# Products of high and low parts, ordered by kind within each group of twelve

## What is computed

```python
def first_block(x, ...):                      # layer 1
    h = rms_norm(x, norm_mix_g)
    proj = h @ w_in                           # 1024 -> 8280 columns
    ...
    merged = sigmoid(gate_a) * o_gdn + sigmoid(gate_b) * o_att
    x = x + merged @ w_out                    # gated delta rule and sparse attention before it
    h2 = rms_norm(x, norm_mlp_g)
    x = x + square(relu(h2 @ w_mlp_up)) @ w_mlp_down
# layer 2: x = x + (retention and forgetting attention) @ w_out,
#          x = x + cross attention to a memory (w_xq, w_xkv, w_xo),
#          x = x + (gated MLP with w_gate, w_up, w_down)
```

## Time and profile before

| what | value |
|---|---|
| median of three runs | 920.71 us (919.72 to 921.14) |
| the profiled execution's own time | 920.04 us |
| its span, first to last instruction | 918.2 us |
| time around the span | 1.8 us |
| TensorE matmuls busy | 899.7 us, 98% of the span |
| TensorE weight loads busy (beside matmuls) | 766.8 us, 84% |
| DVE, ACT, POOL busy | 586.3, 447.9, 113.5 us |
| the 16 DMA engines' mean busy share | about 50% (q1 48.0%) |
| granted TensorE clock, mean over the span | 1.000 |

### The profile page before, as it was taken

The page is one execution under the profiler, slowest core; times in us unless marked ns, Lnnn a source line. Parts: engine busy times, 40 slices in busy tenths (PEclk is TensorE's granted clock), DMA queues, the critical chain, the costliest instruction groups (busy, mean ns, idle before and its releaser), DMA issues.

```text
span 918.2 us, 12609 instructions
## 1 busy us (share of the span) xinstructions
PE 899.7 (98%) x5039; PEld 766.8 (84%) x5039; DVE 586.3 (64%) x834; ACT 447.9 (49%) x632; POOL 113.5 (12%) x83
## 2 busy tenths in 40 slices
PE   8999999999999999999999999999999999999998
PEld 6887787888978999988878889888877888888886
DVE  5378978996686566644356747877765565554542
ACT  6265446854545555533344336545553454444431
POOL 0331225756110000000000002100100000000200
PEclk9999999999999999999999999999999999999999
DMA  8774542344235555555567535524440565554562
GB/s 279 200 249 138 183 138 81 130 123 115 91 102 175 172 181 180 187 190 188 183 202 272 190 94 185 183 93 138 173 148 18 168 195 188 188 183 143 188 220 69
DMA packets 83554, 149.74 MB, mean 163 GB/s; under 512 B 8480, under 2 KB 16208, under 8 KB 83376
## 3 DMA queue, kind: packets, MB, share of 16 engines
q1 hardware_dynamic: 80352, 144.55, 48.0%
q10 hardware_dynamic: 2528, 3.63, 1.1%
q0 software_dynamic: 624, 0.87, 0.8%
HBM read 147.59 MB, written 1.44 MB: 162 GB/s over the span
## 4 chain that ended last, share of the span: by engine, by line
PE 83%; DVE 10%; ACT 3%; DMA 2%; issue 1%; POOL 0%; DVEq 0%; SPq 0%; ACTq 0%
PE gemm L504 21%; PE gemm L506 20%; PE gemm L505 20%; DMA raw<-in_w_in_dram 2%; PE mixbank L642 2%; DVE mix L1893 2%; PE mixbank L617 2%; PE gemm L946 2%; PE mixbank L946 2%; PE gemm L948 2%; PE mixbank L947 2%; PE mixbank L948 2%; PE gemm L947 2%; DVE w_lo L1664 2%; PE mixbank L520 1%
## 5 line engine op out<-in xcount | busy, mean ns | idle before, releaser
L1664 DVE TENSOR_TENSOR w_lo<-raw,w_hi 128x2048 fp32r<-128x2048 f32 (+3 forms) x131 | 284.7, 2183 | 190.6 <-ACT w_hi L1152 190.5
L1152 ACT ACTIVATE w_hi<-raw 128x2048 fp32r<-128x2048 f32 (+3 forms) x140 | 255.2, 1832 | 177.3 <-DMA raw<-in_w_in_dram 51.7
L504 PE MATMUL gemm<-w_hi,s_hi 128*128 128x512 f32 (+3 forms) x784 | 302.5, 386 | 6.4 <-DVE s_lo L1701 2.8
L506 PE MATMUL gemm<-w_hi,s_lo 128*128 128x512 f32 (+3 forms) x784 | 296.0, 378 | 0.0
L505 PE MATMUL gemm<-w_lo,s_hi 128*128 128x512 f32 (+3 forms) x784 | 295.7, 377 | 0.0
L504 PEld LDWEIGHTS gemm<-w_hi,s_hi 128*128 128x128 f32 x784 | 147.5, 188 | 35.9 <-issue 6.8
L506 PEld LDWEIGHTS gemm<-w_hi,s_lo 128*128 128x128 f32 x784 | 147.3, 188 | 27.4
L505 PEld LDWEIGHTS gemm<-w_lo,s_hi 128*128 128x128 f32 x784 | 147.5, 188 | 26.0 <-issue 0.5
L2398 POOL TENSOR_TENSOR sm<-sm 128x2 f32<-128x2 f32 (+4 forms) x13 | 22.7, 1749 | 498.0 <-DVE sm L1708 315.1
L2392 POOL TENSOR_TENSOR w_lo<-raw,w_hi 128x2048 fp32r<-128x2048 f32 x9 | 41.3, 4604 | 158.7 <-ACT w_hi L1152 158.7
L504 PE MATMUL gemm<-w_hi,hT_hi 128*128 128x512 f32 x128 | 50.6, 396 | 0.0
(11 more groups left out here) (333 smaller groups left out, 1190.7 us busy)
## 6 DMA issues: line engine op xcount, KB each, us to landing
raw<-in_w_in_dram SPq DMA_DIRECT2D x40, 1024.0 KB, 5.0
raw<-in_w_mlp_up_dram SPq DMA_DIRECT2D x16, 1024.0 KB, 5.3
raw<-in_w_mlp_down_dram SPq DMA_DIRECT2D x16, 1024.0 KB, 5.1
raw<-in_w_gate_dram SPq DMA_DIRECT2D x10, 1024.0 KB, 5.1
raw<-in_w_up_dram SPq DMA_DIRECT2D x10, 1024.0 KB, 5.0
raw<-in_w_down_dram SPq DMA_DIRECT2D x10, 1024.0 KB, 5.0
raw<-in_w_out_dram SPq DMA_DIRECT2D x8, 1024.0 KB, 5.0
raw<-in_w_xkv_dram SPq DMA_DIRECT2D x8, 1024.0 KB, 5.2
```

Source lines behind the costliest of these rows:

```text
L504: nc.tensor.matmul(o, hi, wh, start=kt == 0, stop=False)
L506: last = nc.tensor.matmul(o, lo, wh, start=False, stop=kt == blk["kt"] - 1)
L1152: nc.scalar.activation(w_hi[:, n % SLOTS, 0:kn, 0:width], raw[:, n % SLOTS, 0:kn, 0:width], ACT.Copy)\
L1664: V.tensor_tensor(w_lo[:, s, 0:kn, 0:width], raw[:, s, 0:kn, 0:width], w_hi[:, s, 0:kn, 0:width].bitcast(F32), ALU.subtract)\
```

## The change

Only TensorE's stream is changed; every matmul of before is still there, with the same operands, and the loads and the streams of ACT, DVE, POOL and SP are the same.

- In `mm`, with activations just turned (`turned`): the pair waits for `w_hi` (`split_hi` or `first_hi`) and for `turn_hi`, makes its four x_hi w_hi; then waits for `w_lo` and makes its four x_hi w_lo; then waits for `turn_lo` and makes its four x_lo w_hi.
- In `mm` otherwise: at a chunk's first pair it waits for `split_hi`, makes four x_hi w_hi and four x_lo w_hi, then waits for `w_lo` and makes four x_hi w_lo. The hidden activations' low parts are waited for at the start, as before.
- The last pair of the blocks in `EARLY` keeps the order of before.
- In the first `up`, the first chunk is done in two groups of 24 (each pair of k tiles with four column tiles), with the kinds in order and with waits for `turn_hi` and `turn_lo`; it still waits for `w_lo` at its start.

```diff
--- before.py
+++ after.py
@@ -484,28 +484,63 @@
                     c = 2 * pair // CK
                     n = blk["chunk0"] + c
                     kn, width = chunk_shape(b, c)
-                    if b == 0:
-                        pe.wait_ge(sem("split_lo" if pair % 2 else "first_lo"), c + 1)
-                    elif 2 * pair == CK * c:
-
-                        pe.wait_ge(sem("split_lo_pool" if pool_chunk(b, c) else "split_lo"), at(low_parts(b, c), 4, i))
-                    if turned is not None:
-
-                        pe.wait_ge(sem("turn_lo"), turned - KT // 2 + pair + 1)
-                    if hidden is not None:
-
-                        pe.wait_ge(sem(hidden), pair + 1)
                     early = b in EARLY and 2 * pair == blk["kt"] - 2
                     tiles = [(kt, t) for kt in (2 * pair, 2 * pair + 1) for t in range(NT)]
-                    for kt, t in sorted(tiles, key=lambda tile: tile[1]) if early else tiles:
-                        o = G[b % 2][t][:, 0:width]
-                        hi, lo = (s[:, kt, P * t:P * t + P] for s in stat)
-                        wh, wl = (s[:, n % SLOTS, kt - CK * c, 0:width] for s in (w_hi, w_lo))
-                        nc.tensor.matmul(o, hi, wh, start=kt == 0, stop=False)
-                        nc.tensor.matmul(o, hi, wl, start=False, stop=False)
-                        last = nc.tensor.matmul(o, lo, wh, start=False, stop=kt == blk["kt"] - 1)
-                        if early and t == 0 and kt == blk["kt"] - 1:
-                            last.then_inc(sem("first_tile"), 1)
+
+                    def product(kt, t, low_x=False, low_w=False):
+
+                        lhs = stat[low_x][:, kt, P * t:P * t + P]
+                        rhs = (w_lo if low_w else w_hi)[:, n % SLOTS, kt - CK * c, 0:width]
+                        return nc.tensor.matmul(G[b % 2][t][:, 0:width], lhs, rhs, start=kt == 0 and not (low_x or low_w),
+                                                stop=kt == blk["kt"] - 1 and (low_x if ends_low_x else low_w))
+
+                    def low_weights():
+
+                        if b == 0:
+                            pe.wait_ge(sem("split_lo" if pair % 2 else "first_lo"), c + 1)
+                        elif 2 * pair == CK * c:
+                            pe.wait_ge(sem("split_lo_pool" if pool_chunk(b, c) else "split_lo"), at(low_parts(b, c), 4, i))
+
+                    ends_low_x = True
+                    if turned is not None:
+                        if b == 0:
+                            pe.wait_ge(sem("split_hi" if pair % 2 else "first_hi"), c + 1)
+                        elif 2 * pair == CK * c:
+                            pe.wait_ge(sem("split_hi"), n + 1)
+                        pe.wait_ge(sem("turn_hi"), turned - KT // 2 + pair + 1)
+                        for kt, t in tiles:
+                            product(kt, t)
+                        low_weights()
+                        for kt, t in tiles:
+                            product(kt, t, low_w=True)
+                        pe.wait_ge(sem("turn_lo"), turned - KT // 2 + pair + 1)
+                        for kt, t in tiles:
+                            last = product(kt, t, low_x=True)
+                    elif early:
+                        low_weights()
+                        if hidden is not None:
+
+                            pe.wait_ge(sem(hidden), pair + 1)
+                        for kt, t in sorted(tiles, key=lambda tile: tile[1]):
+                            product(kt, t)
+                            product(kt, t, low_w=True)
+                            last = product(kt, t, low_x=True)
+                            if t == 0 and kt == blk["kt"] - 1:
+                                last.then_inc(sem("first_tile"), 1)
+                    else:
+                        ends_low_x = False
+                        if 2 * pair == CK * c:
+                            pe.wait_ge(sem("split_hi"), at(n + 1, 4, i))
+                        if hidden is not None:
+
+                            pe.wait_ge(sem(hidden), pair + 1)
+                        for kt, t in tiles:
+                            product(kt, t)
+                        for kt, t in tiles:
+                            product(kt, t, low_x=True)
+                        low_weights()
+                        for kt, t in tiles:
+                            last = product(kt, t, low_w=True)
                     if kt == CK * c + kn - 1:
                         last.then_inc(sem("mm_done"), 1)
 
@@ -939,20 +974,34 @@
                     pe.wait_ge(sem("ev0"), at(B_UP + b - 1, 2, i))
                     pe.wait_ge(sem("ev1"), at(B_UP + b - 1, 2, i))
 
+                def tile_product(kt, f, low_x=False, low_w=False):
+                    n = blocks[B_UP + b]["chunk0"] + kt // CK
+                    w = (w_lo if low_w else w_hi)[:, n % SLOTS, kt % CK, P * f:P * f + P]
+                    return nc.tensor.matmul(UP_BANKS[b % 2][f][:, 0:SEQ], w, (s_lo if low_x else s_hi)[:, kt, :],
+                                            start=kt == 0 and not (low_x or low_w), stop=kt == KT - 1 and low_x)
+
                 def tile_products(kt, f):
-                    n = blocks[B_UP + b]["chunk0"] + kt // CK
-                    o = UP_BANKS[b % 2][f][:, 0:SEQ]
-                    wh, wl = (w[:, n % SLOTS, kt % CK, P * f:P * f + P] for w in (w_hi, w_lo))
-                    nc.tensor.matmul(o, wh, s_hi[:, kt, :], start=kt == 0, stop=False)
-                    nc.tensor.matmul(o, wl, s_hi[:, kt, :], start=False, stop=False)
-                    return nc.tensor.matmul(o, wh, s_lo[:, kt, :], start=False, stop=kt == KT - 1)
+                    tile_product(kt, f)
+                    tile_product(kt, f, low_w=True)
+                    return tile_product(kt, f, low_x=True)
 
                 pe.wait_ge(sem("split_lo"), at(low_parts(B_UP + b, 0), 4, i))
-                for kt in range(CK):
-                    if first and kt % 2 == 0:
-                        pe.wait_ge(sem("turn_lo"), 12 - KT // 2 + kt // 2 + 1)
-                    for f in range(4):
-                        last = tile_products(kt, f)
+                if first:
+
+                    for pair in range(CK // 2):
+                        tiles = [(kt, f) for kt in (2 * pair, 2 * pair + 1) for f in range(4)]
+                        pe.wait_ge(sem("turn_hi"), 12 - KT // 2 + pair + 1)
+                        for kt, f in tiles:
+                            tile_product(kt, f)
+                        for kt, f in tiles:
+                            tile_product(kt, f, low_w=True)
+                        pe.wait_ge(sem("turn_lo"), 12 - KT // 2 + pair + 1)
+                        for kt, f in tiles:
+                            last = tile_product(kt, f, low_x=True)
+                else:
+                    for kt in range(CK):
+                        for f in range(4):
+                            last = tile_products(kt, f)
                 last.then_inc(sem("mm_done"), 1)
                 pe.wait_ge(sem("split_lo"), at(low_parts(B_UP + b, 1), 4, i))
                 if first:
```

## The result

The changed kernel takes **912.93 us** (median of 912.50, 912.81, 913.05 and 914.11); before, four runs on the same chip gave a median of 920.92. The ratio is 0.9921, with a 95% interval of 0.9909 to 0.9933: 7.3 us faster, between 6.2 and 8.4. (The two medians alone differ by 8.0, inside that interval.) The forecast was 913.6 us with a range of 911.0 to 917.0. The profiled execution took 913.05 us with a span of 911.3 (forecast 912.9 and 911.1), against 918.2 before.

A forecast was written before the change was run, and what follows sets the result against it. TensorE, with matmuls busy 98% of the span, bounds the kernel. Stalls won, 5.04 + 2.26 - 0.2 = 7.1 us, take the profiled 920.04 to 912.9; the runs' median lies 0.67 higher, so 913.6 us, range 911.0 to 917.0.

The forecast's parts named there:

- What one stall costs: On TensorE, a stall costs its idle time plus 0.16 us of row overlap, used behind transposes too.
- low activations: At seven TensorE waits for `s_lo`, stalls go whole except at 275.27, where 0.82 is won; 5.04 us in sum.
- Low weights: At two TensorE waits for `w_lo`, 1.11 us is won at 47.76 and 1.15 at 110.58; 2.26 in sum.
- What lies behind: Loads and later work move forward with TensorE; only about 0.2 us is lost in the first attention groups.
- Edits that cost nothing: In TensorE's stream, 161 more waits, alternating banks and neighbours without a shared stationary x_hi cost 0.
- The sum: Over the whole kernel, 5.04 + 2.26 - 0.2 = 7.1 us is won.
- Rival 1: Gains before the attention groups (120 to 262 us) are swallowed: 2.9 us lost, 4.2 left, 916.5 us; chance 0.12.
- Rival 2: Each added wait at a group's fifth and ninth matmul costs; at 0.07 us each, 924.9 us; chance 0.04.
- Rival 3: Matmul distance depends on order: 930.1 us if slower (chance 0.04), 908.4 if faster in MLP down projections (0.03).
- Rival 4: Only one kind of stall is won; without low weights, 915.7 us; chance 0.07, shared with no difference for unseen reasons.

The follow-up runs named there:

- Experiment 1: Kernel before with the new order and waits only for just turned activations (first up block included); 915.25 us, ratio 0.9945.
- Experiment 2: Kernel before with the new order and late low-weight wait only in groups without just turned activations, first up block unchanged; 918.65 us, ratio 0.9979.
- experiment 5: The changed kernel run again unaltered; 914.08 us, ratio 0.9924 to the kernel before.
- experiment 8: The change with five of POOL's eleven small loads of gains issued later, behind its second low part; 912.95 us, ratio 0.9917 to the kernel before.
- experiment 6: The change with kinds ordered over whole chunks (8 x_hi w_hi, 8 low x, wait, 8 low weights); 912.91 us, ratio 0.9918 to the kernel before.
- experiment 9: Two runs on the change: one more low weight part made by POOL, 913.41 us; that plus chunk-wide order, quarter block ahead of POOL's wait and later small loads, 921.66 us.
- experiment 3: The change's order of products with every wait back at its group's start; 920.58 us, ratio 0.9999 to the kernel before.
- experiment 4: Kernel before with two more waits, on a semaphore long met, in each group of twelve products; 920.89 us, ratio 1.0003.
- Experiment 7: Two runs: the change with a quarter of block B_Q + 1 ahead of POOL's wait, 913.35 us; kernel before with late low weights only from B_Q on, 919.48 us.

## Why the prediction held, and where it did not

**What one stall costs, and low activations: right, slightly too small.** At the six places where no other wait follows, the stall went as a whole. Idle plus 0.16 fits where a product of the same kind stands ahead: at 47.76 the lead jumps by 1.17, as forecast. It was 0.05 short at 9.66, behind another kind of matmul, and 0.07 to 0.10 short at the five behind transposes of `x` or `mix`: 0.71, 0.65, 0.99, 0.71 and 0.73 won against 0.64, 0.57, 0.89, 0.63 and 0.63. The rows of the change tell why:

```profile
562.74 0.82 PE L555 MATMUL mixbank<-cst,mix 128*128 128x128 f32 x6
563.32 1.17 PE L494 MATMUL gemm<-w_hi,s_hi 128*128 128x512 f32 x4
```

The transposes' row ends at 563.56 and the product begins at 563.32: an overlap of 0.24, not of 0.16. The step that was off in size is "I use this for the stalls behind transposes too". The same row answers a smaller point: four products behind transposes last 1.17, four in the middle of a stream 1.07 (109.06). The 0.07 to 0.10 that the second product is late by comes behind transposes without any stall too, so it can't be read as the price of a wait. At 275.27 the rest is held by `s_hi` as forecast (0.34 idle in the new row, forecast 0.4). Experiment 1 shows this part alone: 5.2 us of span against a forecast of 5.04.

**Low weights: right in sum, wrong inside.** Experiment 2 gives 1.7 us of span against 2.26 - 0.2, and 0.2 of the 1.7 is the tenth place's. At 47.76 the forecast rest of 0.06 is 0.35. The eight products last 1.1 us and `w_lo` follows `w_hi` by 1.41; I set TensorE's start against the old time of `w_hi` and did not carry the 0.86 won before it, which brings TensorE to the chunk earlier than its load follows. Here "the loads wait for `mm_done`, so they move forward with TensorE" failed: the load is asked for earlier and lands when the small loads let it (experiments 5 and 8). The order over whole chunks removes the rest (experiment 6). That 0.82 came near the forecast is luck in part: when the change was run again TensorE came 0.3 earlier, the load landed 0.5 later (45.1 and not 44.6 us), TensorE stood idle for 0.64 until `w_hi` was there, and the place gave 0.02.

**What lies behind: right mechanism, wrong size, and one wait overlooked.** Of what was won before 120 us 0.34 was lost in the attention groups where I forecast 0.2, and the row maxima came first at 121.03, not 122.75. They moved by 1.72. My rule for it (what was won before the stall, plus DVE's idle 0.53) gives 1.21 + 0.53 = 1.74; I had put 1.97 for what was won, but 0.35 was lost at the weights (0.06 of it forecast), 0.29 at a wait for POOL, and 0.17 was missing from the start. I had not named that wait: TensorE's transposes at 68.48 stand behind POOL's L2489, idle for 0.69 now. POOL's chain started 1.47 us earlier (59.85 against 61.32) and ended 1.21 earlier, for a reason that the rows show. Before:

```profile
62.13 2.29 DVE L1664 TENSOR_TENSOR w_lo<-raw,w_hi 128x2048 fp32r<-128x2048 f32 x1 [0.99 <-ACT w_hi L1152]
65.55 2.41 DVE L1664 TENSOR_TENSOR w_lo<-raw,w_hi 128x2048 fp32r<-128x2048 f32 x1 [1.12 <-ACT w_hi L1152]
```

```profile
62.21 2.41 POOL L2431 TENSOR_TENSOR mix<-mix,cst 128x72 f32<-128x72 f32 x1
```

```profile
65.89 2.27 POOL L2435 TENSOR_TENSOR mix<-mix 128x72 f32<-128x72 f32 x1
```

In the change, DVE's second `w_lo` and the POOL instruction beside it:

```profile
64.01 2.29 DVE L1713 TENSOR_TENSOR w_lo<-raw,w_hi 128x2048 fp32r<-128x2048 f32 x1 [1.01 <-ACT w_hi L1201]
```

```profile
64.05 2.45 POOL L2480 TENSOR_TENSOR mix<-mix,cst 128x72 f32<-128x72 f32 x1
```

POOL's chain is twelve instructions on 72 elements a partition, about 0.34 us each; one that runs beside a `w_lo` of DVE takes 2.3 to 2.5 and ends 0.20 behind it. In each of the fourteen traces two of the twelve are held up so. In the kernel before the second one held is the ninth, in the change the eighth. DVE's second `w_lo` ended 1.66 earlier, as much as TensorE was early there, but POOL had one instruction more left to do behind it. In experiments 6 and 8 it is the sixth, with six left, and the wait for POOL is longer for it. My reason for the rule was wrong though: not DVE's unbroken work is the chain, but TensorE, eviction, `w_hi`, `w_lo` (experiment 9).

**Edits that cost nothing: shown.** Order and met waits, each alone, differ from before by 0.01% and 0.03%, less than can be measured (experiments 3 and 4).

**The sum.** 7.1 was forecast and 7.12 measured by place (6.90 and the 0.22 of the later first matmuls). The closeness is luck in part: 0.43 more at five places behind transposes, 0.05 more at 9.66, 0.14 more at 110.58 (0.08 of it because the second product had stood 0.31 behind the first there, and does not now) and 0.18 at the tenth place, which I had missed, stand against 0.05 less at 275.27 and 0.72 less at 47.76, at POOL's wait and in the attention groups.

**Rivals.** Rival 1 was right in kind and small in size: 0.34 of 2.50 was lost at the attention groups, not all. Experiment 7 makes it 0.6 of 1.25 when the stall at 110.6 is taken alone. Rivals 2 and 3 fall with experiments 4 and 3. Rival 3's two distances, 232 and 224 ns, are a count of rows in a window; from start to start they are 233 and 227, which the edit left as they were. Rival 4 falls with experiments 1 and 2: both kinds work.

**Open.** POOL's hold-up beside DVE's `w_lo` is read from the traces; no run moved one against the other on purpose at that place. Moving ACT's `w_hi` ahead of the eviction, which the chain in experiment 9 suggests, was not tried. The gains of single places come from one execution each. Those from 275 us to 728 repeat within 0.02 us in experiment 1; those before 120 us don't, as 47.76 shows.

## What to carry to other kernels

When an operand arrives in two steps, do first the work that needs only the first step, and put each wait where its operand is used: in the dense stream of this kernel a met wait and another order of accumulating matmuls were free, and a stall shorter than the work put in front of it goes as a whole. The price of a stall is its idle time plus the overlap that the two rows would have without it, read for that pair of instructions. Time won in front of a chain on another engine only counts if the chain is released by what moved: ask which instruction of the moved engine starts it, and whether a load on its way shares the DMA engines with something that could come later. Where DVE and POOL work side by side, look for short instructions of one that last as long as a long one of the other: an extra piece of work for the idle one of the two can hold up the busy one.
